# Decoder layer with two half-FFNs and a convolution mixer: the mixer's residual is added by an accumulating DMA, the second input tile is fetched later, and the last down projection is split in halves for four blocks only

## The reference

```python
h = h + 0.5 * swiglu(rmsnorm(h, ffn1_norm), ffn1_w_gate, ffn1_w_up, ffn1_w_down)   # D_FF = 2816
u = rmsnorm(h, mix_norm)
z = u @ w_in                                             # 7 x 1024 columns
a_val, a_gate, b_B, b_C, b_x, g_a, g_b = jnp.split(z, SPLITS, axis=-1)
a = causal_depthwise_conv(a_val * sigmoid(a_gate), a_dw_w) + a_dw_b     # width 31
y_a = silu(layernorm(a, a_ln_g, a_ln_b)) @ a_w_out
y_b = (b_B * causal_depthwise_conv(b_C * b_x, b_conv_w)) @ b_w_out      # width 3
h = h + (sigmoid(g_a) * y_a + sigmoid(g_b) * y_b) @ w_o
h = h + 0.5 * swiglu(rmsnorm(h, ffn2_norm), ffn2_w_gate, ffn2_w_up, ffn2_w_down)
return rmsnorm(h, final_norm)
```

## Time and profile before

| | |
|---|---|
| median of three runs | 3161.51 us |
| lowest of them | 3161.02 us |
| profiled execution | 3157.62 us, its span 3156.1 us on the slowest core |
| spans of the eight cores | 3136.4 to 3156.1 us, granted clock 0.987 to 0.990 |
| busy share | PE 96%, DVE 78%, ACT 28%, POOL 6% |
| moved by DMA | 615 MB, 195 GB/s |

### The profile page before, as it was taken

How to read it: one execution, slowest core, us unless ns; L and a number is a source line. 1 busy time by engine, 2 the same in 40 slices (tenths; PEclk the granted TensorE clock), 3 DMA queues, 4 the chain that set the end, 5 groups by cost and what they waited for, 6 DMA issues and landing times.

```text
span 3156.1 us, 45091 instructions; the slowest of 8 cores (3136.4 to 3156.1 us)
## 1 busy us (share of the span) xinstructions
PE 3036.5 (96%) x13885; PEld 1387.5 (44%) x14160; DVE 2461.9 (78%) x3458; ACT 876.5 (28%) x1572; POOL 197.0 (6%) x374
## 2 busy tenths in 40 slices
PE   7989999999999999979999999999999999999997
PEld 3434444444444444434444444444444444444445
DVE  2368999969996788858899889879898999896332
ACT  2222233223321224213241233232422332232221
POOL 1111001001110000000001000100000000000000
PEclk8999999999999999989999999999999999999998
DMA  9999959879999799995646555754656555645453
GB/s 185 185 220 195 251 162 193 211 206 209 167 212 256 229 226 234 226 263 189 221 151 196 185 175 176 213 177 149 216 157 221 186 165 187 202 161 186 146 187 123
DMA packets 183241, 615.26 MB, mean 195 GB/s; under 512 B 20896, under 2 KB 23072, under 8 KB 177248
## 3 DMA queue, kind: packets, MB, share of 16 engines
q1 hardware_dynamic: 134288, 432.11, 42.6%
q0 software_dynamic: 47200, 177.99, 28.8%
q10 hardware_dynamic: 1520, 2.27, 0.2%
HBM read 623.78 MB, written 103.81 MB: 231 GB/s over the span
## 4 chain that ended last, share of the span: by engine, by line
PE 75%; DMA 19%; DVE 2%; issue 2%; SPq 1%; ACT 0%; DVEq 0%; POOL 0%; ACTq 0%; POOLq 0%
PE ps L412 75%; DMA wbf<-wslot 9%; DMA wslot<-wpack 4%; DMA hst<-hs 3%; DVE acc L412 1%; DMA hs<-hst 1%; SPq L412 1%; DMA wslot<-wbf 1%; DMA hT<-xT 1%; DMA hs<-hT 0%; DVE hT L412 0%; DVE rstdX L412 0%; ACT sq L412 0%; DMA outT<-hT 0%; ACT L412 0%
## 5 line engine op out<-in xcount | busy, mean ns | idle before, releaser
L412 DVE SCALAR_TENSOR_TENSOR acc<-abuf,vecs_sb,acc 128x512 f32<-128x512 f32 x1920 | 1435.8, 749 | 132.7 <-ACT acc L412 8.9
L412 PE MATMUL ps<-uF,wslot 128*128 128x512 bf16 x5516 | 1246.9, 381 | 35.9 <-DMA wslot<-wpack 10.9
L412 PEld LDWEIGHTS ps<-uF,wslot 128*128 128x128 bf16 x5632 | 551.6, 98 | 708.1 <-issue 56.0
L412 PE MATMUL ps<-uM,wslot 128*128 128x512 bf16 x3517 | 793.4, 379 | 14.5 <-DVE acc L412 5.1
L412 PE MATMUL ps<-act,wslot 128*128 128x512 bf16 (+1 forms) x2938 | 628.6, 368 | 16.4 <-DMA wslot<-wpack 7.5
L412 ACT ACTIVATE fp<-ps 128x512 f32<-128x512 f32 x513 | 304.0, 595 | 1096.7 <-PE ps L412 1053.9
L412 PEld LDWEIGHTS ps<-uM,wslot 128*128 128x128 bf16 x3584 | 350.5, 98 | 436.9 <-issue 17.4
L412 PEld LDWEIGHTS ps<-act,wslot 128*128 128x128 bf16 x2992 | 293.7, 98 | 333.5 <-issue 20.9
L412 DVE TENSOR_TENSOR act<-fp,ps 128x512 bf16<-128x512 f32 x352 | 239.7, 682 | 216.9 <-PE ps L412 201.4
L412 ACT ACTIVATE sq<-hT 128x512 bf16<-128x512 f32 (+1 forms) x260 | 157.8, 612 | 599.2 <-DVE hT L412 570.9
L412 PE MATMUL ps<-acc,wslot 128*128 128x512 bf16 x1008 | 239.5, 381 | 3.8 <-DMA wslot<-wpack 2.9
(11 more groups left out here) (46 smaller groups left out, 934.5 us busy)
## 6 DMA issues: line engine op xcount, KB each, us to landing
wslot<-wbf SPq DMA_DIRECT2D x470, 512.0 KB, 4.6
wslot<-wpack POOLq DMA_DIRECT2D x170, 512.0 KB, 14.4
wslot<-wbf SPq DMA_DIRECT2D x203, 352.0 KB, 3.4
wbf<-wslot SPq DMA_DIRECT2D x80, 512.0 KB, 11.2
wslot<-wpack POOLq DMA_DIRECT2D x61, 352.0 KB, 11.9
hst<-hs POOLq DMA_DIRECT2D x59, 256.0 KB, 6.1
outT<-hT POOLq DMA_DIRECT2D x14, 1024.0 KB, 6.7
wslot<-wbf SPq DMA_DIRECT2D x48, 256.0 KB, 3.7
```

The lines of the kernel that those rows point to most:

```text
L412: ins = getattr(E, meth)(*a, **kw)
```

## The change

- The result of `w_o`, tiles 0 to 6: ScalarE halves it into one of the four `thg` tiles (which also hold the tanh of the gates), and a DMA on POOL's queue adds it to `hs` in DRAM (`stage_add`). The residual is no longer loaded, and VectorE has no step there.
- The four `hst` buffers all serve the normalised tile, in turn, and the first four pieces are loaded at once.
- The second input tile is fetched once the planner's clock of TensorE has reached 50 us.
- `last_down` does blocks 0 to 3 for all 512 tokens, then 4 to 7 for the first half and 7 to 4 for the second. The slabs of the last four stay in their buffers. The scaling of the first half is interleaved with the second half's blocks.
- Half of the final stores go to POOL's queue instead of ScalarE's.

```diff
@@ -135,6 +135,7 @@
+X1_NS = 50000.0
...
@@ -275,11 +276,12 @@
-        self.eng[queue].dma_start(out=out_ap, in_=in_ap).then_inc(self.sem[semkey], 16)
+        kw = {} if accum is None else {"accum_op": accum}
+        self.eng[queue].dma_start(out=out_ap, in_=in_ap, **kw).then_inc(self.sem[semkey], 16)
...
@@ -529,18 +531,21 @@
-    def stage_load(self, t, k, side):
-        i = 2 * side + self.st_i[side] % 2
-        self.st_i[side] += 1
+    def stage_load(self, t, k):
+        i = self.st_i % NST
+        self.st_i += 1
...
-    def stage_store(self, t, k, r, i):
-        self.tr.dma(self.hq(), "sst%d" % i + self.hq(), self.b_hs[t][k], r, self.hs[t, :, k, :], self.stage[i][:], kb=256)
+    def stage_add(self, t, k, y, added):
+        self.tr.dma("pool", "sst%d" % (k % 4), self.b_hs[t][k], y, self.hs[t, :, k, :], y.ap, kb=512, accum=ALU.add)
+        added[0] += 1
+        if k == KC - 1:
+            self.m_out.add(t)
...
@@ -770,13 +775,13 @@
-        for k in range(2):
-            S[k] = self.stage_load(t, k, 0)
+        for k in range(NST):
+            S[k] = self.stage_load(t, k)
...
-            if k + 2 < KC:
-                S[k + 2] = self.stage_load(t, k + 2, 0)
+            if k + NST < KC:
+                S[k + NST] = self.stage_load(t, k + NST)
...
@@ -871,6 +875,8 @@
+            if q == 1 and tr.t["pe"] < X1_NS:
+                return
...
@@ -958,63 +964,78 @@
+        steps = [((0, 1), d) for d in range(KC // 2)] + [((0,), d) for d in range(KC // 2, KC)] + \
+                [((1,), d) for d in reversed(range(KC // 2, KC))]
+        tail = []
+        for es, d in steps:
...
+            if es == (1,):
+                if d == KC - 1:
+                    self.flush(tr.ready([sq]) - 1.0)
+                    assert seen[0] == KC
+                    tail = self.last_scale(t, 0, bh[0], rst[0], nps[0])
+                for _ in range(1 if d == KC - 1 else (2 if d > KC // 2 else 0)):
+                    tail.pop(0)()
         self.flush()
-        self.last_scale(t, 1, bh[1], rst[1], nps)
+        for fn in tail + self.last_scale(t, 1, bh[1], rst[1], nps[1]):
+            fn()
...
             if k % 2 == 1:
-                p = (2 * NT - 1) % NH
-                tr.dma("sp" if k % 4 == 1 else "act", "fin%d" % ((k // 2) % 2), self.b_out, x[k - 1],
+                tr.dma("sp" if k % 4 == 1 else "pool", "fin%d" % ((k // 2) % 2), self.b_out, x[k - 1],
...
@@ -1176,30 +1197,17 @@
+        added = [0]
         for i in range(KC):
-            yield ("wo", lambda: max(tr.ready(mm), tr.ready([S[i][0]])) if i in S else INF)
-            hst, si = S.pop(i)
+            yield ("wo", lambda: max(tr.ready(mm), self.w_ready(t, "wo", i // 2)) if added[0] >= i - 3 else INF)
             sbuf, st = self.slab(t, "wo", i // 2)
             ci = i % 2
             ps = self.bank()
             self.group(ps, [(st[:, (ci * 8 + k) * 128:(ci * 8 + k + 1) * 128], sbuf, mm[k]) for k in range(KC)])
-            tr.op("dve", lambda E: E.scalar_tensor_tensor(
-                out=hst.ap, in0=ps.ap, scalar=0.5, in1=hst.ap, op0=ALU.mult, op1=ALU.add),
-                reads=[ps, hst], writes=[hst], cost=690)
-            self.defer(tr.ready([hst]), lambda i=i, hst=hst, si=si: put(i, hst, si))
+            y = self.r_th.next()
+            tr.op("act", lambda E: E.activation(out=y.ap, in_=ps.ap, func=AF.Copy, scale=0.5),
+                  reads=[ps], writes=[y], cost=600)
+            self.defer(tr.ready([y]), lambda i=i, y=y: self.stage_add(t, i, y, added))
```

More of the change, by code:

```diff
@@ L960, in last_down @@
             rst[e].w, rst[e].r = self.b_rsX.w, list(self.b_rsX.r)
[L961 to L977, removed]
-                tr.op("dve", lambda E: E.scalar_tensor_tensor(
-                    out=x.ap, in0=ps.ap[:, 0:H], scalar=0.5, in1=x.ap, op0=ALU.mult, op1=ALU.add),
-                    reads=[ps, x], writes=[x], cost=450)
-                sq = self.new_sq()
-                tr.op("act", lambda E: E.activation(out=sq.ap[:, 0:H], in_=x.ap, func=AF.Square),
-                      reads=[x], writes=[sq], cost=410)
-                def stat(n=n, sq=sq, nps=nps):
-                    tr.op("pe", lambda E: E.matmul(nps.ap[:, 0:H], lhsT=self.ones[:], rhs=sq.ap[:, 0:H],
-                                                   start=(n == 0), stop=(n == KC - 1)),
-                          reads=[self.b_ones, sq], writes=([nps] if n == 0 else []), cost=MM_NS / 2)
-                    nps.w = ("pe", tr.cnt["pe"])
-                    nps.tw = tr.t["pe"] + 200.0
-                self.late.append((tr.ready([sq]), stat))
-                if e == 1 and n == 0:
@@ L1002, in last_scale, with root, one @@
         H = T // 2
-        sd = self.r_f.next()
-        tr.op("act", lambda E: E.activation(out=sd.ap[:, 0:H], in_=nps.ap[:, 0:H], func=AF.Sqrt, bias=EPS, scale=1.0),
-              reads=[nps], writes=[sd], cost=420, actset="sqrt")
-        self.release(nps)
-        tr.op("dve", lambda E: E.reciprocal(out=rst.ap, in_=sd.ap[:, 0:H]), reads=[sd], writes=[rst], cost=1700)
-        V = self.vecs
-        for k in range(KC):
-            tr.op("dve", lambda E, k=k: E.scalar_tensor_tensor(
+        V = self.vecs
+        p = (2 * NT - 1) % NH
+        def root():
+            sd = self.r_f.next()
+            tr.op("act", lambda E: E.activation(out=sd.ap[:, 0:H], in_=nps.ap[:, 0:H], func=AF.Sqrt, bias=EPS, scale=1.0),
+                  reads=[nps], writes=[sd], cost=420, actset="sqrt")
+            self.release(nps)
+            tr.op("dve", lambda E: E.reciprocal(out=rst.ap, in_=sd.ap[:, 0:H]), reads=[sd], writes=[rst], cost=1700)
+        def one(k):
+            tr.op("dve", lambda E: E.scalar_tensor_tensor(
                 out=x[k].ap, in0=x[k].ap, scalar=V[:, V_FINAL + k:V_FINAL + k + 1], in1=rst.ap,
@@ L1013, in last_scale @@
             if k % 2 == 1:
[L1014 to L1015 removed]
+                tr.dma("sp" if k % 4 == 1 else "pool", "fin%d" % ((k // 2) % 2), self.b_out, x[k - 1],
                        self.outT[t, :, k - 1:k + 1, e * H:(e + 1) * H],
                        self.hT[p][:, k - 1:k + 1, e * H:(e + 1) * H], extra_reads=[x[k]], kb=256)
+        return [root] + [lambda k=k: one(k) for k in range(KC)]
     def store_h1(self, q, t, h, d):
```

61 lines of the change are left out of this document (39 added, 22 removed).

## The result

The changed kernel takes 3206.63 us in the median of three runs, where the kernel before took 3161.51; the ratio is 1.0141, 95% interval [1.0123, 1.0159]. Here and in the experiments, runs in which the cores of one die showed a lower granted clock are left out. The forecast of 3131 us was wrong in sign, and 3207 lies outside its range. The profiled execution took 3206.6 us (span 3204.8) where that of before took 3157.6, so 49 us are to be found (48.7 between the spans). Less than 2% is "same" by the bound of the prediction; the interval shows that it is a loss.

A forecast was written before the change was run, and what follows sets the result against it. TensorE, busy 96%, bounds the kernel, so only its holes can be gained. 19.4 + 10 + 3 + 4 - 6 = 30 us off the profiled 3157.6 gives 3127.6, median 3131 us; range 3109 to 3150 (chance 0.62).

The forecast's parts named there:

- Late tiles therefore cost nothing on TensorE: Accumulations from 2100 us on: landing in 4.0 to 8.9 us, under 12.7 us, so no TensorE loss.
- the 2 us for each early one: Accumulations of tiles 0 to 2: landing about 12.6 us, 2 us lost a tile, 6 in all, ends 0 and 24.
- the threshold of 12.7 us: Accumulation landing time from which TensorE stands still: 5.7 us until ScalarE stops plus 7 us of spare banks.
- Rival A: Accumulations land late at each tile's fifth ScalarE copy, kernel slower; decides from 14.9 us in all tiles; chance 0.16.
- 19.4 us from the residual's holes: Stretches 600 to 700 and 1400 to 1500 us: holes hanging on residual loads close, 11.0 + 8.4 us gained.
- rival B: Holes move instead of closing: only the residual's 19 us gained, some 12 lost again, 3155 us; chance 0.14.
- staging four deep, +10: Normalised-tile loads over four buffers: holes at 1300 to 1400 and 2000 to 2100 us half closed, 10 us, ends 0 and 20.
- one of the forecast's signs of being wrong: New holes of 5 us or more where staged loads are used.
- the x tile, +3: Second x tile fetched later: tile 0's last piece up to 8 us sooner, 3 us gained net, ends 0 and 7.
- the last down projection, +4: Slab reload gone, 7.0 us gained, 3 lost in the chain of output stores; net 4, ends 6 and -0.5.
- The end at Z + 16.7: Eighth last store ends 16.7 us after Z, the last step `hT<-ps`, with 2.8 us a store on POOL; before, Z + 13.7.
- The 3.2 us: Skill's estimate for a 256 KB accumulation counted both ways; by it no wait would arise and the 6 us fall away.

The follow-up runs named there:

- e9_late: The changed kernel with accumulation for tiles 3 to 6 alone, VectorE's residual in the other tiles, staging two deep: 1.008 of the kernel before.
- e5_depth2: The changed kernel with the normalised tile staged two pieces deep instead of four: 1.0103 of the kernel before.
- e6_ring6: e5_depth2 with the two freed staging buffers added to the four copy tiles, making a ring of six: 1.0126 of the kernel before.
- e15_early_gate: e11_early with the gate and the told landing times: 1.0008 of the kernel before.
- e11_early: The changed kernel with accumulation for tiles 0 to 2 alone, VectorE's residual in the others, staging two deep: 1.0078 of the kernel before.
- the gate: Changed kernel; w_o block given out only when its copy's tile comes free, planner told landings come 10 us (early) or 4 us (late) later: 1.0073 of before.
- e16_gate_two: The full changed kernel with the gate, the told landing times and staging two deep: 1.0024 of the kernel before.
- e1_x1: The kernel before with the later second x tile and nothing else: 1.0002 of the kernel before.
- e2_down: The kernel before with the new last down projection and nothing else: 1.0002 of the kernel before.
- e13_own_buf: e2_down with a semaphore and tracked piece for each of the eight last stores, so none waits for another: 0.9974 of the kernel before.
- e4_store: The changed kernel with a plain store in place of each accumulating DMA, the residual left out of the result: 1.0063 of the kernel before.
- e7_hold: The changed kernel, staging four deep, with no slab load between a tile's accumulations on POOL: 1.0135 of the kernel before.

## Why the prediction was wrong

**Failed: "Late tiles therefore cost nothing on TensorE", and the 2 us for each early one.** The terms were 0 and 6 us; by 3000 us TensorE lost 44 us more, gains included. The mechanism (the fifth copy waits for a landing) was there, and the landings lay inside the bounds, at their upper ends. What failed is the threshold of 12.7 us, up to which a stopped ScalarE was free. It counted only TensorE's spare banks. What stands behind the stopped copy also counts: squares and conv starts on ScalarE, and on POOL, which waits for the copies, slab loads and staged loads; and so does the whole-tile load that waits for the last accumulation. e9_late shows it at a late tile, where only 5.37 us were TensorE's wait for a copy and 14.29 came by the long way. In the kernel after, 19 of the 44 us are in tiles that were to cost nothing, some 10 still with staging two deep (e5_depth2). For the early tiles the length of the copy's wait does not even follow the loss: e6_ring6 took it away and gained nothing, e15_early_gate had twice that of e11_early and lost almost nothing; what followed the loss there is VectorE's wait for staged pieces. Rival A had the right side and one of the places, but with a deciding point of 14.9 us in all tiles; late ones lost at 8.7.

**Failed: 19.4 us from the residual's holes.** VectorE's wait for the residual went, its work did not come sooner: the stretch from 600 lost 17 instead of 11, that from 1400 lost 4 instead of 8, and the waits for DRAM pieces add to 66.8 us, 64.7 before. This is rival B, and it took back the gain while A added its cost.

**Wrong sign: staging four deep, +10.** The hole at 2000 closed, but one of the same kind opened at 1734 (VectorE waits for staged pieces, TensorE 6.28 us for squares), one of the forecast's signs of being wrong, and late staged loads last 13.0 us. Four loads at once also head the chain through SP in tile 1. Two deep is better by 0.5% with the gate (e16_gate_two); without it the 0.4% of e5_depth2 lie inside its interval.

**Right in mechanism, zero in sum: the x tile, +3.** The first feed-forward matmul starts at 22.96 us, 3.5 sooner than the 26.44 of before, not before 22; up to 500 us both lose 55 in all, since what the start gained went at 100 to 200 us (15 instead of 11), and e1_x1 is 1.0002. The ends had 0.

**Mis-sized: the last down projection, +4.** No TensorE wait for a slab at the end, as said. The end at Z + 16.7 was Z + 25.5: the first store began 2.0 us later than taken (Z - 1.6), eight took 22.8 us to the last landing (3200.5) instead of 20.3, and 4.3 us lay between that landing and the span's end. Gained 7.0, lost 11.5 in the profiled runs; e2_down says 0 within 0.14%. (The term's lower end was set at -0.5; by its own figures, 7.0 less 21.5 - 13.7, it is -0.8.)

**The price of a transfer.** The accumulations landed in 4.4 us at best and 10.9 in the median. The 3.2 us, an estimate from the Trainium skill, "DMA: Bandwidth & Descriptors", anatomy on the gpsimd path, were reached by none. A second page would have spoken for rival A: the Trainium skill, "Collectives: The Full Stack", section on the bandwidth ceiling, says of ReduceScatter that its add needs two source reads and that it runs at half the rate of AllGather, which copies. It does not speak of a kernel's own DMA; for the late tiles the landings have about that ratio, 8.7 us against 4.6, and early, where the engines are full either way, it is 15.2 against 12.3.

**What stays open.** How much of the gate's gain is the gate and how much the told landing time; they were not tried apart. And the halves do not add up at the same depth: less the 4.5 us of the new end, which each carries, the profiled spans of e9_late and e11_early are 22 us longer each, that of e5_depth2 31.5. The late tiles lost 31 us in e9_late and some 10 in e5_depth2. The whole order is planned anew each time, so such a difference is in part the plan's; no run takes it apart.

## What to carry to other kernels

When an engine starts to wait for a transfer, price everything that stands behind it in its queue, and in the queue that waits for it, not only the consumer's spare buffers. In a kernel whose order is planned, put the measured landing time into the planner before judging the change: here that and the gate turned +1.4% into +0.7% with the same transfers, and staging two deep made it +0.2%. A chain of output stores at the end is on the path in full; eight dependent ones cost more than the reload they replaced. And compare with the smallest kernel that has the gain: without e13_own_buf one would credit the accumulation with what the independent stores brought.

## What the runs showed of the hardware

- An accumulating DMA of 256 KB takes POOL 845 ns to issue, a plain one 542, and lands 4 us later in the median when the DMA engines are half busy (8.7 against 4.6, the kernel after and e4_store).
- With four 256 KB loads in flight, late ones landed in 10.3 to 13.0 us in six runs (medians), with two in 5.8 to 8.2 in seven. Early, while weights are cast, depth does not decide alone: four deep gave medians from 9.6 (e7_hold) to 18.7 us, two deep 8.7 to 11.4.
- Where the last store is POOL's, the span ends some 3 to 4 us after its landing (3200.5 to 3204.8 in the kernel after, about 3145.1 to 3148.0 in e13_own_buf); before, with ScalarE's queue last, it was 0.3 us (3153.6 + 2.2 to 3156.1). No run takes this apart.
